# Two chained blocks on one core: where the SBUF buffers of the float32r products begin

## The reference

```python
def first_block(x, ...):
    h = rmsnorm(x, ln1_g)
    b_a, c_a, x_a, x_b, g_b, gate_a, gate_b = split(h @ w_in)      # 7 x 1024 columns
    y_a = b_a * conv3(c_a * x_a)
    y_b = rg_lru(conv4(x_b) + bias) * gelu(g_b)                    # gated linear recurrence
    x = x + (sigmoid(gate_a + ..) * (y_a @ w_out_a) + sigmoid(gate_b + ..) * (y_b @ w_out_b)) @ w_o
    h = rmsnorm(x, ln2_g)
    x = x + (silu(h @ w_ffn_gate) * (h @ w_ffn_up)) @ w_ffn_down   # hidden width 2816
    return rmsnorm(x, final_g)

def second_block(x, ...):
    p = rmsnorm_2(x, norm1_w) @ w_in
    mix = concat(ssd_mixer(...), mlstm_mixer(...))                 # two chunked recurrences
    x = x + mix @ w_out
    x = x + hier_moe(rmsnorm_2(x, norm2_w), ...)                   # 4 groups of 8 experts, top 2
    return rmsnorm_2(x, norm_f_w)
```

## The kernel before

| stage | moving operand | weights |
|---|---|---|
| mixers, direct | `h_hl` 0 | `m_ring` 96 |
| mixers, differences | `m_t` 96 | `m_ring` 96 |
| merge, first tile | `h_hl` 0 | `m_ring` 96 |
| merge, the others | `h_hl` 0, `mg_yb_hl` 0 | `mg_w_hl` 0 |
| output product | `wo_w_hl` 0 | `h_hl` 0 |
| feed-forward, direct | `h_hl` 0 | `ff_ring` 0 |
| feed-forward, differences | `ff_t` high and low 224 | `ff_ring` 0 |
| feed-forward, down | `ff_down_hl` 224 in slots 0 to 4, 0 in slot 5 | `ff_act_hl` 224 |
| projections, direct | `h_hl` 0 | `pc_ring` 0 |
| projections, differences | `pc_t` high 0, low 32 | `pc_ring` 0 |
| gate columns | `h_hl` 0 | `pg_hl` 32 |
| projections, rows | `pj_w_hl`, `pj_w_slot` 0 | `h_hl` 0 |
| SSD output | `w_hl` 0 | `sd_y_hl` 224 |
| mLSTM output | `h_hl` (there the output weights) 0 | `ml_y_hl` 128 |
| experts | `ex_w_hl`, `h_hl` 0 | `ex_x_hl`, `ex_act_hl` 0 |

## Time and profile before

### The profile page before, as it was taken

How to read it: one execution, slowest core, us unless ns; L and a number is a source line. 1 busy time by engine, 2 the same in 40 slices (tenths; PEclk the granted TensorE clock), 3 DMA queues, 4 the chain that set the end, 5 groups by cost and what they waited for, 6 DMA issues and landing times. The chain is left out here.

```text
span 3342.7 us, 38475 instructions
## 1 busy us (share of the span) xinstructions
PE 3080.4 (92%) x13910; PEld 2506.0 (75%) x13910; DVE 2119.4 (63%) x2539; ACT 1596.0 (48%) x2275; POOL 674.9 (20%) x553
## 2 busy tenths in 40 slices
PE   6999999899999999999899999979868759999994
PEld 4777777687878888788778886767767648888883
DVE  6668677634354545434467776449666389999996
ACT  6544444412343333324444443334354248888883
POOL 4222222100132222000232221134132111111100
PEclk9999999999999999999899999989989869999997
DMA  3222232433222222634253443342153069999995
GB/s 90 70 83 77 84 104 74 158 126 98 104 76 76 95 76 76 227 104 162 75 129 101 117 110 101 109 187 107 70 185 123 32 235 391 394 386 379 381 375 228
DMA packets 374222, 516.06 MB, mean 154 GB/s; under 512 B 66832, under 2 KB 267536, under 8 KB 373040
## 3 DMA queue, kind: packets, MB, share of 16 engines
q1 hardware_dynamic: 355392, 463.49, 40.4%
q0 software_dynamic: 18672, 50.49, 4.1%
HBM read 441.41 MB, written 89.26 MB: 159 GB/s over the span
## 5 line engine op out<-in xcount | busy, mean ns | idle before, releaser
L3701 DVE TENSOR_TENSOR h_hl<-ex_stage,h_hl 128x1024 fp32r<-128x1024 f32 x256 | 305.1, 1220 | 37.8 <-ACT h_hl L3697 35.7
L3697 ACT ACTIVATE h_hl<-ex_stage 128x1024 fp32r<-128x1024 f32 x256 | 271.4, 1060 | 91.0 <-DMA ex_stage<-in_exp_w_up_dram 29.9
L421 PE MATMUL m_ps<-m_t,m_ring 128*128 128x512 f32 x432 | 173.3, 401 | 11.0 <-DVE m_sga L834 4.5
L422 PE MATMUL m_ps<-m_t,m_ring 128*128 128x512 f32 x432 | 169.6, 393 | 0.0
L423 PE MATMUL m_ps<-m_t,m_ring 128*128 128x512 f32 x432 | 169.4, 392 | 0.0
L3701 DVE TENSOR_TENSOR ex_w_hl<-ex_stage,ex_w_hl 128x1024 fp32r<-128x1024 f32 x128 | 154.7, 1232 | 6.0 <-ACT ex_w_hl L3697 5.7
L679 ACT ACTIVATE m_ring<-m_sums 128x512 fp32r<-128x512 f32 x108 | 67.7, 627 | 167.2 <-POOL m_sums L655 113.5
L3697 ACT ACTIVATE ex_w_hl<-ex_stage 128x1024 fp32r<-128x1024 f32 x128 | 134.7, 1054 | 24.5 <-PE ex_ps_g L423 13.4
L421 PE MATMUL ff_ps<-ff_down_hl,ff_act_hl 128*128 128x512 f32 x352 | 138.7, 394 | 4.7 <-DVE ff_down_hl L1571 3.7
L422 PE MATMUL ff_ps<-ff_down_hl,ff_act_hl 128*128 128x512 f32 x352 | 138.1, 392 | 0.0
L423 PE MATMUL ff_ps<-ff_down_hl,ff_act_hl 128*128 128x512 f32 x352 | 137.9, 392 | 0.0
(11 more groups left out here) (626 smaller groups left out, 9172.6 us busy)
## 6 DMA issues: line engine op xcount, KB each, us to landing
ex_stage<-in_exp_w_gate_dram SPq DMA_DIRECT2D x128, 512.0 KB, 5.4
ex_stage<-in_exp_w_up_dram SPq DMA_DIRECT2D x128, 512.0 KB, 5.5
ex_stage<-in_exp_w_down_dram SPq DMA_DIRECT2D x128, 512.0 KB, 5.5
m_stage<-in_w_in_dram SPq DMA_DIRECT2D x56, 512.0 KB, 5.2
ff_down_raw<-in_w_ffn_down_dram SPq DMA_DIRECT2D x44, 512.0 KB, 3.6
pc_stage<-in_w_in_dram SPq DMA_DIRECT2D x36, 512.0 KB, 5.2
ff_stage<-in_w_ffn_gate_dram SPq DMA_DIRECT2D x22, 512.0 KB, 3.7
ff_stage<-in_w_ffn_up_dram SPq DMA_DIRECT2D x22, 512.0 KB, 5.0
```

The costliest lines, as they stand in the source:

```text
L421: nc.tensor.matmul(out, w_hl[0], x_hl[0], start=first, stop=False, skip_group_check=further)
L422: nc.tensor.matmul(out, w_hl[0], x_hl[1], start=False, stop=False, skip_group_check=further)
L3697: nc.scalar.activation(w_hl[u][:, 0], stage[:, s], ACT.Copy).then_inc(s_hi, 1)
L3701: nc.vector.tensor_tensor(w_hl[u][:, 1], stage[:, slot(e, u)], f32(w_hl[u][:, 0]), ALU.subtract).then_inc(s_lo, 1)
```

## The change

It moves buffers; nothing else. The instructions of every engine, their order, their shapes, their waits and their DMAs are word for word those of before. Only addresses differ.

`Over` gets a method `even`, which moves its place up to the next multiple of 256. The mixers' buffers from `m_t` on begin at such a place. `first.at`, from which `m_xb`, `m_u` and the merge's stage count, is now a number and no longer the higher of two, so `m_xb` and `m_u` lie 1,248 bytes lower. The feed-forward's differences and slots count down from a multiple of 256. In the projections the gap ahead of `pc_t_raw` grows from 32 to 256 bytes, and the small conv weights and biases find other places. `sd_y_hl` and `ml_y_hl` are taken from the stack ahead of the other tensors of their stages, so that they start at a multiple of 256.

After it every buffer in the table has remainder 0. (The router's small product, of `rt_w_hl` and `n4_h_hl`, stays at 224 and 96.) Some buffers that feed no float32r product move too: `m_stage`, `m_sums`, `m_g`, `m_cx` and the first block's rows go from 96 to 0, `m_xb` from 0 to 32, `m_u` from 32 to 64, `m_gate_w` from 128 to 32; and `ff_act_raw` and `ff_down_raw` of slots 0 and 1 stay at 224 while what is split from them goes from 224 to 0.

```diff
+BANKS = 256
+
 class Over:
...
+    def even(self):
+        self.at = -(-self.at // BANKS) * BANKS
+        return self
...
-    under = Over(nc, left.at, left.at + 4 * KH * HALF * 4)
+    under = Over(nc, left.even().at, left.at + 4 * KH * HALF * 4)
     first.T = left.take("m1_t", [P, 2, 4, KH, HALF], F32R)
...
-    left.at = first.at = max(left.at, nc.sbuf_base + 15 * KT * P * 8)
+    first.at = nc.sbuf_base + 15 * KT * P * 8
+    assert left.at <= first.at
...
-    first.raw_at = room_at - 4 * t_bytes
+    first.raw_at = room_at // BANKS * BANKS - 4 * t_bytes
...
-        raw_at = w2_at + KT * HALF * 8 + 32
+        raw_at = w2_at + KT * HALF * 8 + BANKS
...
-        g_hl, gstage, cw = tail.take("pg_hl", [P, 2, KT, NG], F32R), tail.take("pg_stage", [P, KT, NG]), tail.take("pc_conv_w", [P, NCV, K])
-        early = Over(nc, late.small_at, late.small_at + P * 4)
-        cb, og = early.take("pc_conv_b", [P, NCV]), early.take("pc_gain", [P, NO])
+        g_hl, gstage = tail.take("pg_hl", [P, 2, KT, NG], F32R), tail.take("pg_stage", [P, KT, NG])
+        cw = Over(nc, late.small_at, late.small_at + P * 4).take("pc_conv_w", [P, NCV, K])
+        between = Over(nc, late.free[0] + 4 * S, late.free[1])
+        cb, og = between.take("pc_conv_b", [P, NCV]), between.take("pc_gain", [P, NO])
...
+        yh = c.sb("sd_y_hl", [P, 2, XT, P], F32R)
         d_row, norm, eps = c.sb("sd_d", [P, H]), c.sb("sd_norm", [P, XT]), c.sb("sd_eps", [P, 1])
...
-        yt, yh = c.sb("sd_yt", [P, XT, P]), c.sb("sd_y_hl", [P, 2, XT, P], F32R)
+        yt = c.sb("sd_yt", [P, XT, P])
...
+        yh = c.sb("ml_y_hl", [P, 2, H, P], F32R)
         neg, ident, last_row, eps = head.neg, head.ident, head.last_row, c.sb("ml_eps", [P, 1])
...
-        yh = c.sb("ml_y_hl", [P, 2, H, P], F32R)
```

## The result

The changed kernel takes 3327.55 us (median of six runs, 3326.09 to 3331.62). The kernel before took 3345.87 us in the six runs that stand beside it (3338.01 to 3353.96). The ratio is 0.994, with a 95% interval of 0.9927 to 0.9954: some 20 us faster. The predicted time was 3314.8 us and the range 3310 to 3325; the measured time lies 2.55 us above the range. The direction and the part that the addresses play were right. Wrong were the level from which the gain was taken off, and the share of it that arrives in the mixers.

A forecast was written before the change was run, and what follows sets the result against it. PE's pace from matmul to matmul was taken to bound the kernel, slowed where operands read together have different remainders by 256. Gains of 21.8 + 2.5 - 0.5 = 23.8 us off 3338.6 gave 3314.8 us, range 3310 to 3325.

The forecast's parts named there:

- The level: Starting time of the whole kernel: 3338.6 us, the median of its runs, from which the 23.8 us gain was subtracted.
- The mixers: Mixers' direct products at even pace: 7.5 us, 8.8 us with the tail on `m_t`, less 0.5 us for ring waits.
- with that row's waits as they are some 0.5; I take 0.5 off: Mixers: PE's seven waits for `m_ring`, 2.9 us, would cost 0.5 us of the gain; far end 5 us.
- The second rival: Weight preparation and chunk loops pace PE in mixers, projections and chunk stages: only 14.7 us gained, 3323.9 us; chance 0.12.
- Feed-forward, down product, projections: Products on differences 8.2 us, down product's slot 5 1.5 us, projections 4.1 us plus 0.2 us for narrow gate matmuls.
- The chunk stages: SSD and mLSTM output products: 2.5 and 1.8 us, together 4.3 us, of which 2.5 us was taken as arriving.
- The pace of the others: Even pace elsewhere not quite 226.7 ns: 0.2 ns for each of 5,000 matmuls, 1 us taken off the gain.
- That the address does nothing: Rival for the whole kernel: the 7 ns comes from other activity at those places, time stays 3338.6 us; chance 0.05.
- That DVE and POOL collide more: Rival in mixers and projections: DVE's splits lengthen, 35 us more work, up to 3350 us; chance 0.03.
- The two rules of the skill: Independent read ports for PE and 16-byte lines in SBUF: by either the address change would do nothing, 3338.6 us.

## Why the prediction was wrong where it was

Against 3314.8 the measured 3327.55 is 12.8 us too long: 7.3 us because the kernel before is slower than the 3338.6 that I started from (3345.87 beside the changed kernel), and 5.5 us because the gain between these two medians is 18.3 and not 23.8.

- **The level, 7.3 us.** The step that failed is the last of the sum: "That execution lies 4.5 us above the median of the runs; nothing in the sum depends on that, so from the median". The three runs shown (3338.57 in the middle) were at the low end of what this kernel does: the six beside the changed kernel have 3345.87, and the 52 beside the experiments 3337 to 3359 with 3349.2 in the middle. The profiled execution was as lucky, with one half-clock stretch in the body of its SSD stage where its repeat has six. With 3345.87 the same sum gives 3322.1, and the measured time lies 5.5 above that; the forecast as a ratio, 0.9929 (3314.8 of 3338.6), lies just within the measured interval. I had taken the spread of three runs for that of the kernel.
- **The mixers, 8.3 us forecast, 3.1 measured.** The step that failed is "with that row's waits as they are some 0.5; I take 0.5 off". The matmuls do save time: the distances of those that follow each other fell by 7.3 us, against 8.8 forecast (6.5 in place of 7.5 on `h_hl`, 0.9 in place of 1.3 behind it). Of this 3.0 us are waited away at seven places: 1.7 in four waits for `m_xb`, 1.3 in three behind the convolution. Another 0.45 goes into the wait for `m_sga`, and 0.3 into the one at 66 us. That leaves 3.5; the clock at the start and the waits of the merge's first tile make 2.9 of it in the first pair of profiles and 3.6 in the second. The second rival had the mechanism for the mixers, and nearly the size (5 of 8.8 lost; 5.2 of 8.3 are missing in the table, 1.5 of them because the distances fell by 7.3 and not 8.8). What it said of the projections and the chunk stages did not come true. I gave it 0.12, because PE had waited for the ring for only 2.9 us, and I left the waits for `m_xb` (2.6 us) and `m_sga` (4.5 us) out of the sum, though the same view shows them. A wait says that there is no room at that place, and its size does not bound what can be lost there: 0.17 us became 0.60. All eight places behind 100 us that took part of the gain had a wait before.
- **Feed-forward, down product, projections:** forecast 14.0, measured 13.7. Here PE is busy nearly throughout (423 of 425 us in the first), and count times distance is the stage's gain.
- **The chunk stages:** forecast 2.5, mean 6.0 over the profiles, but the first pair of profiles alone showed a loss in SSD (200.5 to 201.5 us). The product's own distances fell by 2.2 us in SSD and 1.4 in mLSTM, 3.6 of the 4.3 forecast. The rest goes with the granted clock: with the new addresses no profile has an SSD stage above 205.2 us, with the old ones five of six have, though one of these by only 0.3 us. The kernel with only the chunks' buffers moved points the same way (one profile, 203.5 us; its twelve runs span 11 us, where the three others with twelve runs and the old chunk addresses span 16, 17 and 20). Whether the even pace or the shifted places bring that about is open; no run separates them.
- **Luck in the sum.** That the stages add up to 22.8 us beside 23.8 forecast is no success of the parts: 5.2 us too much in the mixers stand against 3.5 us too little in the chunk stages.
- **The pace of the others,** for which I took off 1 us: the large groups came to 226.5 to 227.9 ns, that of the mLSTM output to 228.7, and the experts did not change. The 48 narrow gate products did not reach it, 230.6 ns after 232.0. Their weight tiles lie 128 bytes apart, so with the buffer at 0 half of them are at remainder 128: what is said of the table, that the remainder of the start is that of the tiles, does not hold for `pg_hl`.
- **The rivals.** That the address does nothing is refuted by the four kernels with one edit or other remainders each. That DVE and POOL collide more did not happen (946 ns for the feed-forward's split, where the earlier trace rows have 986, and 711 and 741 in the mixers and projections, where they have 711 and 740).
- **The two rules of the skill.** By the Trainium skill, page "TensorE: Matmul & The Clock Gate", section "Step-by-step: what each phase is for", the two read ports are independent, and loading weights takes nothing from the running matmul. The runs don't agree with that as a statement on pace: the same stream takes 226.7 or 233.3 ns. The Trainium skill, page "SBUF — State Buffer", section "Specifications (TRN2)", gives lines of 16 bytes; that nothing coarser counts was my reading of it. All of these buffers begin at multiples of 32, and in every pair tried the pace went with the remainder by 256 of one against the other. What in the chip brings that about no run shows. That the weight load and the moving operand get in each other's way is my inference from their running side by side.

## What to carry to other kernels

Where TensorE fills a stage, set the distance between starts beside the addresses of the moving operand and of the weights that load meanwhile: in this kernel unequal remainders by 256 cost 6 to 7 ns for most float32r matmuls of 512 columns, and moving a buffer cost nothing. Before crediting a faster engine with its whole saving, list every wait that it has already, however short and for whichever engine. In the mixers each such place swallowed all that was saved while the other engine's chain ran, and moving one link of that chain passed much of the wait on to the next place. And take the spread of the kernel's times from more than three runs before subtracting from their median; a forecast of the ratio would have stood, at the edge of the measured interval.

## What the runs showed that I had not expected

- A remainder difference of 64 (0 and 192, moving less weights) costs 2.4 ns a matmul, all others tried 5 to 7.5; a difference of 192 (0 and 64) has the full price, so it is not symmetrical. A difference of 96 was tried only in some narrow gate tiles.
- After a run of unequal pairs the next few even ones are slow too, five in the feed-forward of before, seven in the kernel with other remainders; with all pairs even this tail is gone (1003.87 - 1001.83 is nine full-pace steps right behind a change of tile).
- The kernel before scatters by 22 us over 52 runs, the changed one by 5.5 us over eleven. In the profiles that goes with the granted clock of the SSD stage (0.93 at 200.5 us, 0.89 at 209.0 and 210.8): TensorE falls to half clock up to seven times in a stage in which it waits for DVE again and again. What decides in which execution this happens stays open.
